# Decode attention of a hybrid decoder step: a running maximum and value products three steps behind the keys, with the decode exponentials ahead of the prompt's on ScalarE

## The reference

```python
def diff_attend_sample(q, k, v, lam, k_past, v_past):
    scale = q.shape[-1] ** -0.5
    s_past = jnp.einsum('bqhcd,bkhcd->bhcqk', q, k_past).astype(F32) * scale
    s_new = jnp.einsum('bqhcd,bkhcd->bhcqk', q, k).astype(F32) * scale
    s_new = jnp.where(jnp.tril(jnp.ones((T, T), dtype=bool)), s_new, -jnp.inf)
    a = jax.nn.softmax(jnp.concatenate([s_past, s_new], axis=-1), axis=-1)
    w = (a[:, :, 0] - lam * a[:, :, 1]).astype(v.dtype)
    return (jnp.einsum('bhqk,bkhv->bqhv', w[..., :P], v_past)
            + jnp.einsum('bhqk,bkhv->bqhv', w[..., P:], v))
```

## Time and profile before

| what | value |
|---|---|
| median of 3 runs | 1883.73 us (1881.60 to 1884.62) |
| span of the profiled execution | 1880.3 us (its time with what lies around the span was not recorded) |
| PE busy | 1773.0 us, 94% |
| DVE busy | 1192.5 us, 63% |
| ACT busy | 735.6 us, 39% |
| POOL busy | 341.2 us, 18% |
| data moved by DMA | 265.73 MB, mean 141 GB/s |
| attention, first key transposes to last merge | 433.81 to about 867 us |

### The profile page before, as it was taken

How to read it: one execution, slowest core, us unless ns; L and a number is a source line. 1 busy time by engine, 2 the same in 40 slices (tenths; PEclk the granted TensorE clock), 3 DMA queues, 4 the chain that set the end, 5 groups by cost and what they waited for, 6 DMA issues and landing times.

```text
span 1880.3 us, 35481 instructions
## 1 busy us (share of the span) xinstructions
PE 1773.0 (94%) x13062; PEld 1639.1 (87%) x13062; DVE 1192.5 (63%) x1946; ACT 735.6 (39%) x1418; POOL 341.2 (18%) x360
## 2 busy tenths in 40 slices
PE   6999999996999999996999999999999999999998
PEld 6999999984666667665998999999999999999997
DVE  4223742475777777765458876667677878699443
ACT  5113322564655565653225333222323424245320
POOL 1111331001233333332111211211121000000110
PEclk9999999898999999998999999999999999999998
DMA  5323551227999999977111222222222424232121
GB/s 162 108 80 82 141 140 56 61 83 236 330 350 354 346 357 360 353 231 226 35 45 46 80 69 81 81 70 69 81 70 69 157 81 134 74 106 86 47 69 48
DMA packets 232923, 265.73 MB, mean 141 GB/s; under 512 B 16162, under 2 KB 173428, under 8 KB 232756
## 3 DMA queue, kind: packets, MB, share of 16 engines
q1 hardware_dynamic: 211988, 195.36, 33.2%
q0 software_dynamic: 20768, 68.17, 10.7%
HBM read 229.79 MB, written 29.21 MB: 138 GB/s over the span
## 4 chain that ended last, share of the span: by engine, by line
PE 45%; DVE 6%; ACT 1%; issue 1%; DMA 1%; POOL 0%; DVEq 0%; ACTq 0%
PE psum L2518 33%; PE psum L150 10%; DVE x_second_lo L2532 1%; DVE unit_lo L1910 1%; DMA x_first_hi_raw<-scratch_z 1%; PE psum L2197 0%; PE psum L2894 0%; DVE x_second_lo_raw L2536 0%; DVE rstd_and_products L2576 0%; DVE x_first_lo L2532 0%; DVE h L2576 0%; ACT unit_hi L1904 0%; DVE rstd_and_products L2009 0%; DVE x_lo L2226 0%; DMA w_raw<-in_w_ple_gate 0%
## 5 line engine op out<-in xcount | busy, mean ns | idle before, releaser
L2518 PE MATMUL psum<-x_second_hi,unit_hi 128*128 128x364 f32 x924 | 304.5, 330 | 8.0 <-DVE x_second_lo L2532 4.6
L2518 PE MATMUL psum<-x_second_hi,unit_lo 128*128 128x364 f32 x924 | 303.4, 328 | 0.0
L2518 PE MATMUL psum<-x_second_lo,unit_hi 128*128 128x364 f32 x924 | 303.4, 328 | 0.0
L1303 POOL DMA_DIRECT2D dec_v<-in_cache_v x256 | 137.6, 538 | 288.1 <-issue 282.2
L150 PE MATMUL psum<-x_hi,w_hi 128*128 128x364 f32 x768 | 182.0, 345 | 5.8 <-DVE x_lo L2226 5.8
L2518 PEld LDWEIGHTS psum<-x_second_hi,unit_hi 128*128 128x128 f32 x924 | 173.8, 188 | 10.8 <-issue 5.7
L2518 PE MATMUL psum<-x_first_hi,unit_hi 128*128 128x364 f32 x528 | 173.7, 329 | 0.6 <-DVE x_first_lo L2532 0.6
L2518 PEld LDWEIGHTS psum<-x_second_hi,unit_lo 128*128 128x128 f32 x924 | 174.0, 188 | 0.0
L2518 PEld LDWEIGHTS psum<-x_second_lo,unit_hi 128*128 128x128 f32 x924 | 173.7, 188 | 0.0
L2518 PE MATMUL psum<-x_first_hi,unit_lo 128*128 128x364 f32 x528 | 173.5, 329 | 0.0
L2518 PE MATMUL psum<-x_first_lo,unit_hi 128*128 128x364 f32 x528 | 173.2, 328 | 0.0
(11 more groups left out here) (313 smaller groups left out, 3313.3 us busy)
## 6 DMA issues: line engine op xcount, KB each, us to landing
dec_k<-in_cache_k SPq DMA_DIRECT2D x256, 256.0 KB, 5.7
dec_v<-in_cache_v POOLq DMA_DIRECT2D x256, 256.0 KB, 5.5
w_raw<-in_w_in SPq DMA_DIRECT2D x25, 512.0 KB, 3.9
scratch_z<-ffn_hidden SPq DMA_DIRECT2D x22, 546.0 KB, 2.8
w_raw<-in_w_ffn_gate SPq DMA_DIRECT2D x22, 512.0 KB, 3.8
w_raw<-in_w_ffn_up SPq DMA_DIRECT2D x22, 512.0 KB, 3.8
w_raw<-in_w_ffn_down SPq DMA_DIRECT2D x16, 512.0 KB, 4.0
feat_swap<-feat_n SPq DMA_DIRECT2D x32, 136.5 KB, 2.4
```

The costliest lines, as they stand in the source:

```text
L1303: eng.dma_start(ring[:, slot, p:p + 1, :], cache[bass.ds(page, 1)].rearrange("o t f -> t o f")).then_inc(sem, 16)
L2518: ins = pe.matmul(bank[b], w[unit][:, j, :], x[slot][:, j, :], start=start and j == 0 and w is m.uhi and x is m.xhi7, stop=j == k - 1 and ...
```

## The change

LAG becomes 3 and STEPS falls to 68. There is no common maximum any more: for each group a running maximum is kept (`negm`, one column per group, starting from the new tokens' maximum), the exponential of a group uses the running maximum up to it and reads S_BANK directly, and DVE keeps a running output `oacc`, scaled by a factor `fade` = exp(old maximum - new maximum) each time a group's value product is added (`add_output`). At the end the partial sums are weighted by `share` and added. On ACT, `exps(t-2)` now stands between the copies of keys 0 and keys 1, ahead of the weight copy and of the prompt's exponential. The new tokens' scores are made at the first group of a sample instead of behind its last. The next score product waits for the exponential instead of the copy. The rings of keys and values have five slots; POOL loads values 0 at once and 1 to 4 behind key groups 0 to 3. The output weights load when the last unit but one is turned. The four `norm_prompt` stand behind the loop. The new buffers are laid where `dec_s` was.

```diff
-KR, VR, QR, PRE = 4, 4, 4, 3
+KR, VR, QR, PRE = 5, 5, 4, 3
-LAG = NG + 1
+LAG = 3
...
-            b, last = divmod(t - NG, NG)
-            if last == 0 and 0 <= b < DB:
+            b, first = divmod(t - 1, NG)
+            if first == 0 and 0 <= b < DB:
                 use(("new_s", b), "dve")
...
-            sp.wait_ge(s["o_done"], NU)
+            sp.wait_ge(s["turned"], pieces_before(NU - 1))
...
-                if n < VR:
-                    gp.wait_ge(d["ring_filled"], ring.filled(("keys", 2 * n, H - 1)))
-                else:
+                if 0 < n < VR:
+                    gp.wait_ge(d["ring_filled"], ring.filled(("keys", n - 1, H - 1)))
+                elif n:
                     gp.wait_ge(d["pv_done"], n - VR + 1)
...
+            def exps(k):
+                b, g = divmod(k, NG)
+                u = b % 2
+                bias = negm[:, u, g:g + 1]
+                act.wait_ge(d["negm"], k + 1)
+                if k >= 2:
+                    act.wait_ge(d["ring_filled"], ring.filled(("p", k - 2)))
+                if g == 0 and b >= 2:
+                    act.wait_ge(d["final"], 4 * (b - 1))
+                act.activation(m.pg[:, k % 2, :], S_BANK, ACT.Exp, scale=SC, bias=bias,
+                               accum_out=esum[:, u, g:g + 1]).then_inc(d["exp_done"], 1)
                 if g == 0:
                     if b:
                         act.wait_ge(d["ring_filled"], ring.filled(("new_p", b - 1)))
+                    act.activation(m.pn[:, 0:NS], m.sn[:, :], ACT.Exp, scale=SC, bias=bias,
+                                   accum_out=esum[:, u, NG:NG + 1]).then_inc(d["expn_done"], 1)
+                else:
+                    act.activation(fade[:, u, g:g + 1], negm[:, u, g - 1:g], ACT.Exp, scale=-1.0, bias=bias
+                                   ).then_inc(d["fade_done"], 1)
...
             for t in range(STEPS):
-                if 0 <= v < NKV and not first_group:
-                    exps(v)
+                k = t - 2
                 if t < NKV:
                     take_keys(t, 0)
+                if 0 <= k < NKV:
+                    exps(k)
+                    if k % NG == NG - 1:
+                        shares(k // NG)
+                if t < NKV:
                     take_keys(t, 1)
                 if c == 1 and 0 <= n - 1 < NU:
                     copy_weights(n - 1, 0)
                 prompt_exps(t - 1)
-                if first_group:
-                    exps(v)
...
                 if k:
-                    pe.wait_ge(d["s_taken"], k)
+                    pe.wait_ge(d["exp_done"], k)
...
             def max_scores(k):
                 dve.wait_ge(d["s_full"], k + 1)
-                dve.tensor_reduce(mx[:, g:g + 1], S_BANK, AX.X, ALU.max)
+                dve.tensor_reduce(mx, S_BANK, AX.X, ALU.max).then_inc(d["mx_done"], 1)
+                if g == 0:
+                    take_new(b)
+                dve.wait_ge(d["mx_done"], k + 1)
+                before = neg_new if g == 0 else negm[:, u, g - 1:g]
...
+                dve.scalar_tensor_tensor(negm[:, u, g:g + 1], mx, -SC, before, ALU.mult, ALU.min).then_inc(d["negm"], 1)
...
+            def add_output(v):
+                b, g = divmod(v, NG)
+                dve.wait_ge(d["pv_done"], v + 1)
+                if g == 0:
...
+                    dve.tensor_copy(m.oacc, O_BANK[:, 0:DV]).then_inc(d["summed"], 1)
+                else:
+                    dve.wait_ge(d["fade_done"], (NG - 1) * b + g)
+                    dve.wait_ge(d["summed"], v)
+                    dve.scalar_tensor_tensor(m.oacc, m.oacc, fade[:, b % 2, g:g + 1], O_BANK[:, 0:DV], ALU.mult, ALU.add
+                                             ).then_inc(d["summed"], 1)
...
                 if t >= LAG + NG and (t - LAG - NG) % NG == 0:
+                    add_output(v - 1)
                     finalize((t - LAG - NG) // NG)
                 if 0 <= t - 2 < NKV:
                     max_scores(t - 2)
-                if 0 < t - 1 <= NKV and (t - 1) % NG == 0:
-                    take_new((t - 1) // NG - 1)
-                if 0 <= t - 2 < NKV:
-                    copy_scores(t - 2)
+                if 0 < v <= NKV and v % NG:
+                    add_output(v - 1)
...
-                if HALVES < t <= HALVES + H:
-                    norm_prompt(t - HALVES - 1)
+            for h in range(H):
+                norm_prompt(h)
```

More of the change, by code:

```diff
@@ L1218, in attention_memory @@
     o = O_U + 8 * TB + 32
-    m.ss, o = m.at("dec_s", o, [P, PAST + NS])
+    k4, o = m.at("dec_k_more", o, [P, KR - 4, 4, H * P])
+    v4, o = m.at("dec_v_more", o, [P, VR - 4, 4, H * P])
+    m.kr = [kr[:, r] for r in range(4)] + [k4[:, r] for r in range(KR - 4)]
+    m.vr = [vr[:, r] for r in range(4)] + [v4[:, r] for r in range(VR - 4)]
     m.kt, o = m.at("dec_kt", o, [P, 2, H, 4 * PAGE])
+    oo, o = m.at("dec_osc", o, [P, 2, DV])
+    m.oacc, m.osc = oo[:, 0], oo[:, 1]
+    m.sn, o = m.at("dec_s_new", o, [P, NS])
     m.os, o = m.at("dec_os", o, [32, DB, DV])
@@ L1302, in load_pages @@
         page = eng.value_load(ids[0:1, 4 * n + p:4 * n + p + 1], min_val=0, max_val=POOL - 1)
-        eng.dma_start(ring[:, slot, p:p + 1, :], cache[bass.ds(page, 1)].rearrange("o t f -> t o f")).then_inc(sem, 16)
+        eng.dma_start(ring[slot][:, p:p + 1, :], cache[bass.ds(page, 1)].rearrange("o t f -> t o f")).then_inc(sem, 16)
 def load_keys(eng, m, scr, h, part, sem):
@@ L1356, in attention @@
     neg_lam = m.sc[:, 20:21]
-    mx, esum, ssum, cs, negm = (m.sc[:, 24:33], m.sc[:, 34:52].rearrange("p (u g) -> p u g", u=2), m.sc[:, 52:54],
-                                m.sc[:, 54:56], m.sc[:, 56:58])
+    mx, mx_new, neg_new = m.sc[:, 24:25], m.sc[:, 25:26], m.sc[:, 26:27]
+    ssum, cs = m.sc[:, 52:54], m.sc[:, 54:56]
+    negm, esum, fade, share = (m.run[:, :, n, :] for n in range(4))
     def shown(i):
@@ L1470, in take_keys @@
                 act.activation(m.kt[:, t % 2, h, :], ring_bank(("keys", t, h)), ACT.Copy).then_inc(d["ring_act"], 1)
-            def exps(v):
-                b, g = divmod(v, NG)
-                if g == 0:
-                    act.wait_ge(d["negm"], b + 1)
-                    if b >= 2:
-                        act.wait_ge(d["final"], 4 * (b - 2) + 1)
-                act.wait_ge(d["s_taken"], v + 1)
-                if v >= 2:
-                    act.wait_ge(d["ring_filled"], ring.filled(("p", v - 2)))
-                act.activation(m.pg[:, v % 2, :], m.ss[:, 512 * g:512 * g + 512], ACT.Exp, scale=SC,
-                               bias=negm[:, b % 2:b % 2 + 1], accum_out=esum[:, b % 2, g:g + 1]).then_inc(d["exp_done"], 1)
+            def exps(k):
[9 more added lines that the diff above has]
+                               accum_out=esum[:, u, g:g + 1]).then_inc(d["exp_done"], 1)
                 if g == 0:
@@ L1485, in exps, with shares @@
                         act.wait_ge(d["ring_filled"], ring.filled(("new_p", b - 1)))
-                    act.activation(m.pn[:, 0:NS], m.ss[:, PAST:PAST + NS], ACT.Exp, scale=SC,
-                                   bias=negm[:, b % 2:b % 2 + 1], accum_out=esum[:, b % 2, NG:NG + 1]
-                                   ).then_inc(d["expn_done"], 1)
+                    act.activation(m.pn[:, 0:NS], m.sn[:, :], ACT.Exp, scale=SC, bias=bias,
[3 more added lines that the diff above has]
+                                   ).then_inc(d["fade_done"], 1)
+            def shares(b):
+                u = b % 2
+                act.activation(share[:, u, :], negm[:, u, :], ACT.Exp, scale=-1.0, bias=negm[:, u, NG - 1:NG]
+                               ).then_inc(d["share_done"], 1)
             def copy_os(b):
@@ L1586, in turn_keys @@
                 for p in range(4):
[L1587 removed]
+                    ins = pe.transpose(ring_bank(key)[:, p * P:p * P + P], m.kr[t % KR][:, p, h * P:h * P + P], ident)
                 ins.then_inc(d["ring_filled"], 1)
@@ L1641, in values @@
                         ins = pe.matmul(O_BANK[32 * h:32 * h + 32, 0:DV], m.pts[:, v % 2, p, 32 * h:32 * h + 32],
-                                        m.vr[:, v % VR, p, h * P:h * P + P], start=False, stop=g == NG - 1 and p == 3,
+                                        m.vr[v % VR][:, p, h * P:h * P + P], start=g > 0 and p == 0, stop=p == 3,
                                         tile_position=(0, 32 * h), skip_group_check=True)
@@ L1648, in merge @@
                 emptied(("merge", b))
-                pe.matmul(ring_bank(("merge", b))[0:32, 0:DV], const(m, "merge"), m.osc[:, :], start=True, stop=True
+                pe.matmul(ring_bank(("merge", b))[0:32, 0:DV], const(m, "merge"), m.osc, start=True, stop=True
                           ).then_inc(d["ring_filled"], 1)
@@ L1676, in _ @@
                     score(t - 1)
-                if t and t % NG == 0 and t // NG <= DB:
-                    score_new(t // NG - 1)
+                if t % NG == 1 and t // NG < DB:
+                    score_new(t // NG)
                 if 0 <= v < NKV:
```

(2 more changed lines are left out.)

55 lines of the change are left out of this document (30 added, 25 removed).

## The result

The changed kernel takes 1937.08 us (median of 4 runs, 1935.43 to 1938.65), the kernel before beside it 1883.17: the ratio is 1.0284, 95% interval 1.0270 to 1.0298. The forecast was 1911, with a range that ended at 1932. So the direction was right and the size was not: 53.9 us slower, where 27 was forecast. The profiled execution took 1935.43 us around a span of 1933.8.

What follows compares the result with a forecast made beforehand. PE was taken to bound steady-state attention, busy 93.98 of 100.21 us a head. Start +9, steps 10 to 63 +39 and end -21 gave +27 on the 1883.73 median: 1911 us, own range 1898 to 1924, 8 in 10 1889 to 1932.

Steps and rivals of the forecast that it cites:

- (a): End of attention: six fewer drain steps, 20.5 us from step 64 to the next stage instead of 41.6; gain 21 us.
- (b): Start of attention: values now in steps 3 to 8 cost 7 us, page waits before step 4 cost 2; 9 us.
- (c): ACT's chain before the prompt scores: decode exponential 0.72 us plus fade 0.19, 0.91 us longer in every step.
- (d): ACT's decode exponential waits for DVE's running maximum in odd steps only, 0.33 us on average.
- (e): Sequence starts: the old stall moves to steps 8b+3, scores at 6.7 and 6.9 us, plus 3.7 each; +4.0 a head.
- The rival of the clock: PE gaps of 1 to 3 us drop attention to 1.2 GHz for stretches: 1950 us and more; chance 0.02.
- Longer than forecast: DVE later in odd steps or pages late in the first ten steps: 1926 to 1936 us; chance 0.18.
- Score(t-1) waits for the exponential at no cost: The next score product waits for exps(t-2) instead of the copy; that ends before the prompt scores, no cost.
- DVE, SP and POOL don't bind in the steady state: DVE's add_output and running maximum replace its score copy without binding; SP's and POOL's queues carry less per us.
- The hidden rival: ACT's new order costs PE nothing in steady state: 1872 us, or 1852 without sequence-start stalls; chance 0.11.

Runs made afterwards that it cites:

- b1: a2 with the load of the new tokens' values put first in SyncE's queue, ahead of the key pages; 1878.03 us, 0.9970 of the kernel before.
- b2: b1 with value pages of groups 1 to 4 also asked for two key groups later; 1878.95 us, 0.9973 of the kernel before.
- c1: b3 with new tokens' values loaded first and only block 0 of the prompt's values ahead of the keys; 1869.66 us, 0.9929 of the kernel before.
- a1: The kernel before with only its decode exponential moved between ACT's copies of keys 0 and keys 1; 1903.28 us, 1.0104 of the kernel before.
- a2: The changed kernel with exps(t-2), its fade and the shares moved behind the prompt exponential; 1879.83 us, 0.9984 of the kernel before.
- c3: The changed kernel with the decode exponential behind the prompt's only in the seven sequence-start steps; 1919.78 us, 1.0191 of the kernel before.
- a4: The changed kernel with DVE's final_scale, add_output and finalize behind max_scores at a new sequence; 1924.55 us, 1.0210 of the kernel before.
- b3: a2 with ACT copying keys 2 ahead of the decode exponential in seven sequence-start steps; 1870.25 us, 0.9923 of the kernel before.
- b4: b2 and b3 together; 1869.88 us, 0.9928 of the kernel before.

## Why the prediction was right in direction and wrong in size

- *(a) the end*: -17.8 instead of -21. The three drain steps took 14.0 us to the end of the last finalize (917.62 + 0.34 less 903.97), not 12; DVE then waited 1.27 for ACT's root, which I had left out. Mis-sized by 3 us; the mechanism held.
- *(b) the start*: this step failed. I took +2 before step 4, with 6 as the upper bound, and it was +8.5; steps 4 to 8 were +8.4 against 7. I bounded it by the bytes that are asked for ahead of step 4, and did not ask which load the newly moved value product needs and what stands before it in SP's queue: `new_v` behind 2 MB. But the order was only where the wait showed (b1, b2, c1). What grew is what DMA moved, with its busy share at 1.00 and 1.03: 17.1 MB by step 9 before, 24.0 MB in the changed kernel, 5.5 MB of the difference being value pages. At 344 GB/s these are 16 us, an estimate; +16.9 was measured. What is not shown is that they all had to pass. By step 9 the products have used the pages of six groups, 6.3 MB, and 9.7 had been moved, because the ring of five asks ahead. Before, none was used by then and 4.2 had been moved. An unneeded 3.4 MB would be 10 us at that rate, and no run held them back far enough to tell.
- *(c) ACT's order in every step*: right. 0.91 forecast; 3.87 - 3.01 = 0.86 in step 40. The fade measured 0.286 us and 0.18 from its start to the next instruction's, 0.28 and 0.19 forecast. The Trainium skill (ScalarE: Activation LUTs, What ACT_TABLE_LOAD costs) gave the same by its fixed cost and overlap, and these rows agree. a1 shows the order's cost without the rest of the change, a2 the rest without the order. Four even steps of a head paid nothing, as forecast.
- *(d) the wait for DVE*: right, in odd steps only, 0.21 in step 39 (0.33 on average forecast).
- *(e) the sequence starts*: the gap was right within 0.35 us (scores at 7.14 on average, 6.7 and 6.9 forecast), and part of what it missed is the clock. What followed the gap was not in the sum. I had +3.7 us for each start, and the steps grew by 6.1 (12.0 on average, 5.9 before): seven times 2.4 is 17 of the 18.2 us that were missing in steps 9 to 64.
- *The rival of the clock, put at 0.02*: this is the judgement that failed, and the largest part of the miss. I dismissed it with one row (843 to 850, PE busy 4.65 of 7 us at 0.97) and with PE's busy share of about 85%, both averages. The row was misread. It begins in the last 0.4 us of a stretch at half clock, and a gap of 2.14 us in PE's work ends 1.7 us ahead of that stretch, all in the trace of the kernel before:

```profile
838.31 0.33 PE L1616 MATMUL psum<-consts,dec_pn 128*128 128x128 f32 x1 [2.14 <-ACT dec_pn L1486]
...
840.00:843.41 3.41, 3.41 (x40) 3.03 (x35) 0.00 (x0) 0.34 (x2) 1.32 (x3) 0.50 0.72 223
```

From 475 to 840 us there is no other in the kernel before; in the changed one there is one in each sequence start. In step 35 a gap of 2.10 us and one of 1.37 stand around it, with 0.38 us of work between them; the gaps of up to 1.06 us in plain steps are followed by none. The price of the seven, an estimate: the work behind the scores took 34.2 us in these steps, where the undisturbed starts of c3 (2.93 and 3.15 us) make 21.2, and what stands between the last gap and the scores 2.7 more: 15.6 us in all, about 1.6 for a stretch of 3.4 us and 2.5 to 2.9 for one of 6.8. My price for the rival, "1950 and more", was as wrong: I let it act on all of attention, and it acts seven times. I had cited the Trainium skill (TensorE: Matmul & The Clock Gate, Part 1) for the view that only true idleness costs; the runs show gaps of about 2 us in an otherwise busy PE followed by half clock, so that reading of it does not hold here, and neither does the sentence that the row agrees.
- *Longer than forecast, put at 0.18*: the measured 1937 us lies just above its 1926 to 1936, but it is so by luck. Late loads in the first ten steps were some 8 us of the 27 missing; DVE was not later in odd steps than I had set it.
- *Score(t-1) waits for the exponential at no cost*: right, also where it is later (1.0 us in six times in a2). *DVE, SP and POOL don't bind in the steady state*: right (a2).
- *The hidden rival* fell, but its place was the right one: 0.91 us of ACT work a step, ahead of the prompt's exponential or behind it, decides 57 us.

**Open:** what decides whether a gap of about 2 us lowers the clock. At the sequence starts of a2, b1, b2 and c3 the gap is 1.9 or 2.1 us with the same work around it, and 1, 3, 2 and 4 of seven were followed by half clock. In a4 two gaps of 0.85 and 1.37 us close together were, in all seven places, so the length of one gap does not decide it. No run varied the gap by itself. Open too are the value pages of (b), and whether half clock in the first 70 us, where DMA sets the pace, costs anything.

## What to carry to other kernels

Ask of an instruction that moves not how busy its engine is, but what stands behind it in that engine's order and who waits for that; ACT had 40% idle time, and PE paid for the added 0.86 us in full in a step like t=40, and for nothing only where a prompt product kept it busy longer. Where a change delays a step that already has a gap, price the work behind the gap at the lower clock too, and look at every such place by itself rather than at a head's average. Before a row of averages is used against a rival, open the timeline ahead of it: here the row hid the very event. When a use is moved ahead in a stage that starts with transfers, count the bytes that will have been moved by then, those that run ahead of need too, and divide by the measured rate; reordering the queue mostly moved the wait here.

## What the runs showed of the hardware

- A gap of 1.9 or 2.1 us in PE's work at a sequence start was followed by a stretch at 1.2 GHz in ten of 28 places (a2, b1, b2, c3), four of seven within one execution (c3); a single gap of 1.0 or 1.3 us at the same place never was (28 places in b3, b4, c1, c2). Two gaps close together, 0.85 and 1.37 us (a4) or 2.1 and 1.3 to 1.4 us (the changed kernel), were in 14 of 14. Such a stretch of 3.4 us cost 1.63 us in c3.
- The 128x512 exponential takes 0.685 us (changed kernel) or 0.703 (a2) when it reads PSUM, 0.716 (a1) or 0.732 when it reads SBUF (means of 64).
- A 128x1 activation with its bias from memory takes 0.286 us, and ACT's next instruction starts 0.18 us behind its start. It costs the chain less than its duration shows.
- The 128 KB of the new tokens' values landed 20.7 us after their issue behind the 2 MB load (changed kernel), and 2.4 us after it when issued first (b1).
